# Products of ones by ones in TensorE's pauses of a two-block transformer kernel

## The reference, cut to what matters

```python
def first_block(x, ...):            # two layers, each:
    # h = rms_norm(x) @ w_in, split in three mixers
    # mLSTM (4 heads), latent attention (6 heads, rope), chunked spatial gating
    # x = x + rms_norm(mixers) @ w_out
    # x = x + hier_moe(rms_norm(x))
def hier_moe(x, ...):
    # best of 4 groups, then the best 2 of its 8 experts, for each token
    # h = silu(xi @ w1[e]) * (xi @ w3[e]);  y = (h @ w2[e]) * weight
def second_block(x, ...):           # two layers, each:
    # proj = x @ w_in; gated delta rule and gated linear attention, chunk by chunk
    # x = layer_norm(ALPHA * x + o @ w_out)
```

## Time and profile before

| | |
|---|---|
| median of 3 timed executions | 1992.63 us (1990.78 to 1992.74) |
| the profiled execution | 1996.03 us |
| its span, first to last instruction | 1994.2 us |
| TensorE busy | 1892.2 us, 95% of the span |
| mean granted TensorE clock | 0.969 |
| VectorE, ScalarE, GpSimd busy | 774.9, 460.7, 428.7 us |
| chain that ended last | TensorE 84%, DMA 7%, VectorE 5%, ScalarE 2% |

### The profile page before, as it was taken

One profiled execution on the slowest core, in us unless ns is written; L12 is line 12 of the kernel. 1 busy time (PEld: TensorE's weight loads), 2 busy tenths in 40 slices (PEclk: granted clock), 3 DMA queues, 4 the chain that ended last, 5 costly groups with the idle time before them and its releaser, 6 DMA issues.

```text
span 1994.2 us, 24830 instructions
## 1 busy us (share of the span) xinstructions
PE 1892.2 (95%) x9590; PEld 1122.4 (56%) x9590; DVE 774.9 (39%) x1981; ACT 460.7 (23%) x1245; POOL 428.7 (21%) x463
## 2 busy tenths in 40 slices
PE   7999997999996999999899989799999999999998
PEld 4566555555553556655555545354668755466774
DVE  2835335211122463534521111223556332356642
ACT  3333220111112333312011111121232112223221
POOL 0101311334332010230233433100133000013300
PEclk9999897999998999989799999899999999999999
DMA  6121065999965022017799996412002031110201
GB/s 226 37 88 43 0 279 212 387 410 369 384 253 217 34 81 85 1 41 293 261 417 402 416 400 248 174 42 84 33 32 85 1 114 57 71 45 33 85 1 43
DMA packets 52822, 323.33 MB, mean 162 GB/s; under 512 B 20877, under 2 KB 22189, under 8 KB 29921
## 3 DMA queue, kind: packets, MB, share of 16 engines
q1 hardware_dynamic: 33344, 292.28, 37.0%
q0 software_dynamic: 19360, 29.45, 4.1%
HBM read 404.21 MB, written 30.93 MB: 218 GB/s over the span
## 4 chain that ended last, share of the span: by engine, by line
PE 84%; DMA 7%; DVE 5%; ACT 2%; issue 2%; POOL 0%; SPq 0%; POOLq 0%; DVEq 0%; ACTq 0%
PE bank L576 15%; PE bank L941 13%; PE bank L2208 10%; PE bank L2194 9%; PE bank L959 7%; DMA y_rows<-b_va,b_rows_ix 6%; PE bank L588 4%; PE bank L2382 3%; PE bank L2373 3%; PE bank L560 2%; PE bank L923 2%; PE bank L2177 1%; PE bank L663 1%; PE bank L650 1%; PE bank L2289 1%
## 5 line engine op out<-in xcount | busy, mean ns | idle before, releaser
L941 PE MATMUL bank<-b_arena,b_nat 128*64 128x256 f32 x3008 | 347.0, 384 | 8.0 <-DMA b_arena<-in_w,b_over_ix 4.4
L576 PE MATMUL bank<-b_arena 128*128 128x512 f32 (+2 forms) x768 | 313.3, 562 | 4.4 <-issue 2.2
L941 PEld LDWEIGHTS bank<-b_arena,b_nat 128*64 128x64 f32 x3008 | 219.4, 139 | 158.6 <-issue 59.8
L1423 DVE TENSOR_TENSOR b_nat<-bank,b_prm 128x512 f32<-128x512 f32 x94 | 65.1, 693 | 429.4 <-PE bank L923 429.3
L576 PEld LDWEIGHTS bank<-b_arena 128*128 128x128 f32 x768 | 146.4, 196 | 140.1 <-issue 107.3
L2208 PE MATMUL bank<-b_actT,b_ring 128*128 128x512 f32 x512 | 224.0, 594 | 0.0
L959 PE MATMUL bank<-b_arena,b_ebuf 128*64 128x512 f32 x752 | 182.1, 605 | 6.0 <-ACT b_ebuf L1264 6.0
L2194 PE MATMUL bank<-b_ring,b_actT 128*128 128x384 f32 (+1 forms) x512 | 174.5, 497 | 2.4 <-DVE b_actT L3064 2.4
L1396 POOL DMA_INDIRECT y_rows<-b_va,b_rows_ix x94 | 95.6, 1017 | 312.3 <-ACT b_va L1272 286.1
L2208 PEld LDWEIGHTS bank<-b_actT,b_ring 128*128 128x128 f32 x512 | 96.0, 190 | 114.9 <-issue 113.8
L2194 PEld LDWEIGHTS bank<-b_ring,b_actT 128*128 128x128 f32 x512 | 96.8, 193 | 70.5 <-issue 24.7
(11 more groups left out here) (367 smaller groups left out, 2400.4 us busy)
## 6 DMA issues: line engine op xcount, KB each, us to landing
b_arena<-in_w SPq DMA_DIRECT2D x64, 2048.0 KB, 12.6
b_arena<-in_w SPq DMA_DIRECT2D x64, 1024.0 KB, 10.1
b_ring<-in_w_t SPq DMA_DIRECT2D x8, 2048.0 KB, 8.6
b_arena<-in_w SPq DMA_DIRECT2D x8, 1536.0 KB, 9.0
b_ring<-in_w_n2b SPq DMA_DIRECT2D x6, 1536.0 KB, 6.7
b_arena<-in_w_out SPq DMA_DIRECT2D x4, 2048.0 KB, 7.3
b_arena<-y_rows SPq DMA_DIRECT2D x8, 1024.0 KB, 8.0
b_ring<-in_w_out SPq DMA_DIRECT2D x4, 2048.0 KB, 7.7
```

The source lines that it names most:

```text
L576: ins = pe.matmul(bank[:, 0:width], actT[:, k, tok(i)], w[:, k, :], start=k == 0, stop=k == KD - 1)
L941: ins = pe.matmul(psum[2 + b % 2][f * CAP:(f + 1) * CAP, 0:256], xgT[:, b % 2, k % 4, k // 4, :], w[:, k, f, :], start=k == 0, stop=k == K ...
L1423: return dve.tensor_tensor(out, a, b, op)
```

## The change

`idle_products(bank, n)` multiplies the tile of ones by itself n times into the first 128 columns of a bank, each time from scratch. It is called at four places of TensorE's program: 22 times ahead of the first layer, after a wait for `ones`; 16 times in each layer between the wait for the free banks and the first gathered block; and after the last `down` of a layer, 72 times in layer 0 and 55 times in layer 1. That is 181 products. Nobody reads them and no semaphore is raised by them. No other engine's program is changed.

```diff
--- before.py
+++ after.py
@@ -741,6 +741,13 @@
                     ins = pe.matmul(bank[:, 0:RW], actT[:, k, tok(i)], w_r[:, k, :], start=k == 0, stop=k == KD - 1)
                 ins.then_inc(*full)
 
+            def idle_products(bank, n):
+
+                for _ in range(n):
+                    pe.matmul(bank[:, 0:P], ones[:, :], ones[:, :], start=True, stop=True)
+
+            pe.wait_ge(*after(0, "ones", 1))
+            idle_products(psum[0], 22)
             for l in range(L):
                 def x_tile(i):
 
@@ -961,6 +968,7 @@
                                             start=f == 0, stop=f == 1)
                     ins.then_inc(sg.sem("moe_y"), 1)
 
+                idle_products(psum[6], 16)
                 turn_tokens(0)
                 for b in range(NB):
                     up(b)
@@ -974,6 +982,7 @@
                         down(b - 1)
                 turn_hidden(NB - 1)
                 down(NB - 1)
+                idle_products(psum[0], 72 if l < L - 1 else 55)
 
         def run_scalar(act):
             def halves(l, stage, i, gain):
```

## The result

| | before | changed |
|---|---|---|
| median of 22 executions each | 1993.75 us (1988.77 to 1999.23) | 1990.36 us (1987.66 to 1993.56) |
| profiled execution, its span | 1994.2 us | 1990.8 us |
| its mean granted clock | 0.969 | 0.976 |

The ratio is 0.9983, with a 95% interval from 0.9975 to 0.999: the change gains 3.4 us (2 to 5), where 7.2 were forecast. That is real but under half, and inside the 0.2% that I had called no change. The change's profiled execution is itself not typical: the mean granted clocks of the 22 lie between 0.976 and 0.979 (mean 0.978), and its own is at the low end.

The account below looks back on a forecast made before the run. TensorE was taken as the bound, busy nearly throughout, with savings where it alone carried half-clock stretches. Against the median: 1992.6 - 2.3 - 2.0 - 1.4 - 0.4 - 1.1 = 1985.4 us; own range 1982 to 1988, widest 1981.5 to 1990.5.

Parts of the forecast that it names:

- Joints: After the last `down` of each layer: full clock held by products, -2.55 us between layers, -1.9 us between blocks.
- Expert heads: Start of each layer's expert stage: earlier end of first `up`, -2.3 and -0.2 us; against the median -1.4 and -0.4.
- behind the heads each block is six microseconds of TensorE: Expert stage after its head: each block is six microseconds of TensorE work; no loss from a clock fall counted.
- Program head: Before layer 0: 22 products lift the clock; group A gains 2.5 us if held, 0 to 0.8 if fallen; -1.2 taken.
- Rival 1: Clock falls again in holes ahead of N0 and the program's group A; 2.0 and 1.1 us lost, 1988.5; chance 0.22.
- the widest range: Whole kernel: 1981.5 us with all upper ends together, to 1990.5 us, which leaves out the slower case.
- Rival 2: All four places: products of ones neither hold nor lift the clock; together +28 us, 2020; chance 0.06.
- Rival 3: Layer 1's expert stage, DMA share 1.00: earlier savings are taken back there, -2.4 us left, 1990.2; chance 0.10.
- The chance of 0.74: Whole kernel: faster by more than 0.2% (4.0 us), under 1988.6 us; same 0.20, slower 0.06.

Follow-up runs that it names:

- change_hole_filled: The full change plus 4 more products behind the transposes of block 1, in the hole behind the first `up`: 1988.06 us, ratio 0.9973 against the kernel before.

## Why the prediction was wrong

**Joints: right.** 0.112 us a pass was forecast and measured (16.34 us for 144, with a tail of 0.28). -2.55 and -1.9 against -2.45 and -1.86 on the same pair of traces, start of the transposes included (640.33; 641.1 less the 0.86 us by which the products began before 625.0 gives 640.2). The order of the waits was right as well: from the end of the last `down` (625.21 before, 624.21 after) VectorE's eviction starts at 17.0 and 17.2 us, group A at 17.8 and 18.0, the scaling at 20.1 and 20.3, so they stood still as forecast, and that they come 0.8 us sooner in the trace was saved ahead of them. Over all traces, from the end of the last `down` to the second transposes, the joint of the layers takes 23.0 us (mean of six) with nothing put in and 21.1 with the products or transposes, the joint of the blocks 19.9 and 17.7 (six against the seven that held): -1.9 and -2.2, where -2.3 and -2.0 were counted against the median. Alone they measured -3.2 us (-5.2 to -1.2) against -4.3.

**Expert heads: the step that failed.** I counted -1.8 against the median; alone they measured +1.2 (-0.6 to +3.2). The working up to the end of the first `up` was nearly sound: it ended 1.6 us sooner in layer 0 (forecast 1.8 to 2.9) and 0.3 later in layer 1 (0.8 sooner to 0.3 later). It was too low by the 0.2 us between 3.45, the chain's piece up to the next instruction, and 3.67, the whole group as the 6.62 was read. What failed is the sentence that behind the heads each block is six microseconds of TensorE: the fall of the clock there was put at nothing, without a reason. Behind the first `up` come 16 passes of 32 columns, four transposes and a 0.9 us wait. Before the change that stretch stood behind an `up` that began at half clock, and the second `up` was at full clock in all eight heads seen. With the first `up` at full clock throughout, the same stretch lets the clock fall, in three heads of six traced, at 1.7 us each. The products moved the cold place one block on. Filling the holes turned +1.2 into -2.8, of which the granted clocks of the executions put 3.1 us on the falls. Why the stretch is harmless behind the slower `up` no run shows. The second, smaller error is what the delay was set against: I had 5.4 to 6.5 us for 16 products and they took 5.7 to 6.4, but I compared with one profiled execution, whose head in layer 0 was the longest of four (20.7 against 19.1 to 20.6), and took its layer 1 for even; there the pause is a microsecond shorter and 16 lose 0.8.

**Program head: right in kind, its size not shown.** -1.1 forecast, -1.4 measured (-3.4 to +0.4), and both cases, held and fell, showed in traces; the clock held in one of three. With the hole filled it held in all four.

**The sum.** Joints, expert heads and program head alone give -3.2 + 1.2 - 1.4 = -3.4, the change's own figure. The parts add up, and 3.0 of the missing 3.8 us are the expert heads, 1.1 the joints, less 0.3 at the program's head. Each part is uncertain by 2 us, so that they meet the 3.4 to a tenth is luck.

**Rivals.** Rival 1 (the clock falls again behind the products) had the right mechanism at too few places: I named the holes ahead of N0 and of group A at the program's head and gave it 0.22, and passed by the one behind the first `up`. Of the two that I named, the program's head fell in the change's trace and N0's only in a later one. That the measured 1990.4 lies near this rival's 1988.5 and within the widest range is no merit of its working, which took 2.0 from the joint of the blocks, where nothing was lost. Rival 2 is out: products of ones hold the clock and lift it. Rival 3 is neither shown nor refuted. The chance of 0.74 for faster by more than 0.2% took the expert heads' -1.8 as sure in every case: without it the sum is -5.4, and with the measured +1.2 it is -4.2, at the bound of 4.0 us. An edit with a loss on its other side (a delay of the gather's transposes, priced, and a clock that can fall behind them, not priced) should have had a case of its own.

## What to carry to other kernels

Work put in only to keep the clock has to cover the whole stretch up to the next long dense work, narrow passes and short waits included; if it stops short, the cold place can move on to the next thin stretch and take the gain with it. Size it by the pause at the speed that it will run at (at half clock a product is twice as long: ten about fitted a pause of 4.2 to 5.2 us, sixteen outlasted it). And go through every thin stretch behind the one that is repaired: what was harmless behind slow work may not be behind fast work. Where a fall comes only in part of the executions, one trace can show the wrong case; the mean granted clock of all executions tells how often it comes.

## What the hardware showed

- 150 float32 transposes in a row kept the granted clock at full for 16 us, as 144 product passes did.
- Products of ones by ones lift the clock from half: 32 passes take 5.69 to 6.42 us, where all at half would be 6.8 (32 x 0.213) and all at full 3.6. In the ten groups of 32 or 64 passes at the expert heads the granted clock came back 4.0 to 5.5 us after their start, after 18 to 26 passes (change, layer 1: 956.98 to 960.9; change_hole_filled, layer 1: 958.1 to 963.6).
- The same program's clock falls at a given thin stretch in some executions and not in others: behind the first `up` in three of six heads, in block two for a stretch of 3.4 us at 1831 in the changed kernel and at full clock there in the trace of before. This (up to 3.3 us in block two, 1.7 in a head) and layer 1's expert stage, in which TensorE waits for weights and whose length wandered between 284 and 290 us, go a long way towards the 10 us by which single executions of one kernel differ.
- At the very start the clock's view shows full where the rows are at half: 1.00 for 0 to 10 us in the trace of before, whose eight transposes there take 1.97 us.
